# The mean subtraction of three LayerNorm walks moved from GpSimd to VectorE

## The reference

```python
def layernorm(x, g, b):
    mu = jnp.mean(xf, axis=-1, keepdims=True)
    var = jnp.mean(jnp.square(xf - mu), axis=-1, keepdims=True)
    y = (xf - mu) * lax.rsqrt(var + LN_EPS) * g + b

def hybrid_layer(x, ...):
    proj = x @ w_in
    (q_lat, kv_lat, k_rope, g_mla, p_in, g_pool, c_h, c_b, c_c, g_conv) = jnp.split(proj, ...)
    y_mla = mla_mixer(...) * silu(g_mla); y_pool = ...; y_conv = ...
    out = concatenate([y_mla, y_pool, y_conv]) @ w_out + b_out
    return layernorm(DEEPNORM_ALPHA * x + out, ln_g, ln_b)

def first_block(...):
    h = layernorm(x, emb_ln_g, emb_ln_b)
    for l in range(DEPTH):          # DEPTH = 2
        h = hybrid_layer(h, ...)
```

## Time and profile before

| | |
|---|---|
| median of 3 runs | 2504.43 us (2503.02 to 2504.67) |
| profiled execution, its own time | 2505.22 us |
| its span in the trace | 2503.5 us |
| mean granted TensorE clock | 0.986 of full |
| TensorE matmul busy | 2414.2 us (96%) |
| VectorE busy | 1259.9 us (50%) |
| ScalarE busy | 890.3 us (36%) |
| GpSimd busy | 396.5 us (16%) |

### The profile page before, as it was taken

The page is one execution under the profiler, slowest core; times in us unless marked ns, Lnnn a source line. Parts: engine busy times, 40 slices in busy tenths (PEclk is TensorE's granted clock), DMA queues, the critical chain, the costliest instruction groups (busy, mean ns, idle before and its releaser), DMA issues.

```text
span 2503.5 us, 31553 instructions
## 1 busy us (share of the span) xinstructions
PE 2414.2 (96%) x11534; PEld 1977.2 (79%) x11534; DVE 1259.9 (50%) x1794; ACT 890.3 (36%) x1344; POOL 396.5 (16%) x391
## 2 busy tenths in 40 slices
PE   4999999999999999999999999899999999999997
PEld 2888888788888788888788886688878888887886
DVE  8665543366446565444366546635245444444333
ACT  4522222365223522222365223322234444444221
POOL 6400000033003300000042003003002122222000
PEclk8999999999999999999999999999999999999999
DMA  4455554212221455553212222322222222223332
GB/s 141 149 182 169 183 177 133 77 60 67 93 92 67 156 185 170 175 184 126 83 52 68 92 92 101 126 93 93 100 93 68 76 79 80 75 75 100 127 101 75
DMA packets 78280, 277.69 MB, mean 111 GB/s; under 512 B 8832, under 2 KB 9088, under 8 KB 77824
## 3 DMA queue, kind: packets, MB, share of 16 engines
q1 hardware_dynamic: 61344, 213.29, 25.8%
q0 software_dynamic: 16864, 63.45, 7.6%
HBM read 268.31 MB, written 8.39 MB: 111 GB/s over the span
## 4 chain that ended last, share of the span: by engine, by line
PE 80%; issue 9%; DVE 5%; POOL 3%; ACT 2%; DMA 0%; DVEq 0%; ACTq 0%; SPq 0%; POOLq 0%
PE bank L322 25%; PE bank L324 25%; PE bank L323 25%; POOL sum L407 1%; DVE w_lo L317 1%; PE bank L1898 1%; DVE x_lo L1037 1%; POOL probs L394 1%; PE bank L1828 1%; ACT w_hi L294 0%; PE bank L1962 0%; PE bank L1679 0%; PE bank L1680 0%; DVE x_res L1598 0%; PE bank L1963 0%
## 5 line engine op out<-in xcount | busy, mean ns | idle before, releaser
L324 PE MATMUL bank<-x_hi,w_hi 128*128 128x512 f32 x2880 | 1125.6, 391 | 0.0
L323 PE MATMUL bank<-x_hi,w_lo 128*128 128x512 f32 x2880 | 1124.1, 390 | 0.0
L322 PE MATMUL bank<-x_lo,w_hi 128*128 128x512 f32 x2368 | 946.7, 400 | 30.7 <-DVE x_lo L1037 17.2
L317 DVE TENSOR_TENSOR w_lo<-w_raw,w_hi 128x1024 fp32r<-128x1024 f32 (+1 forms) x384 | 483.6, 1262 | 792.7 <-ACT w_hi L294 791.1
L294 ACT ACTIVATE w_hi<-w_raw 128x1024 fp32r<-128x1024 f32 x390 | 407.5, 1048 | 950.6 <-PE bank L324 926.9
L324 PEld LDWEIGHTS bank<-x_hi,w_hi 128*128 128x128 f32 x2880 | 542.0, 188 | 115.3
L323 PEld LDWEIGHTS bank<-x_hi,w_lo 128*128 128x128 f32 x2880 | 543.4, 189 | 107.8 <-issue 2.4
L322 PEld LDWEIGHTS bank<-x_lo,w_hi 128*128 128x128 f32 x2368 | 447.7, 189 | 124.6 <-issue 30.9
L322 PE MATMUL bank<-mix_lo,w_hi 128*128 128x512 f32 x640 | 252.8, 395 | 1.3 <-issue 1.0
L394 POOL TENSOR_SCALAR probs<-probs,stats 128x128 f32<-128x128 f32 (+3 forms) x128 | 138.6, 1089 | 672.7 <-DVE stats L1329 672.6
L322 PEld LDWEIGHTS bank<-mix_lo,w_hi 128*128 128x128 f32 x640 | 120.7, 189 | 27.2 <-issue 1.7
(11 more groups left out here) (304 smaller groups left out, 2268.9 us busy)
## 6 DMA issues: line engine op xcount, KB each, us to landing
w_raw<-stream SPq DMA_DIRECT2D x390, 512.0 KB, 3.5
ada_w<-wada POOLq DMA_DIRECT2D x96, 512.0 KB, 4.6
x_res<-xT SPq DMA_DIRECT2D x16, 256.0 KB, 5.5
x_res_spill<-x_res POOLq DMA_DIRECT2D x8, 512.0 KB, 7.5
x_res<-x_res_spill POOLq DMA_DIRECT2D x8, 512.0 KB, 7.5
outT<-x_res SPq DMA_DIRECT2D x16, 256.0 KB, 2.3
cond_b<-cond POOLq DMA_DIRECT2D x2, 1024.0 KB, 5.2
row_params<-rows POOLq DMA_DIRECT2D x1, 1536.0 KB, 7.5
```

What stands on the lines that cost most here:

```text
L317: nc.vector.tensor_tensor(out=WL[:, slot, :cols[n]], in0=RAW[:, slot, :cols[n]], in1=WH[:, slot, :cols[n]].bitcast(F32), op=ALU.subtract). ...
L322: nc.tensor.matmul(out, wh, xl, start=first, stop=False)
L323: nc.tensor.matmul(out, wl, xh, start=False, stop=False)
L324: return nc.tensor.matmul(out, wh, xh, start=False, stop=last)
```

## The change

VectorE does the subtraction itself, just ahead of its multiplication, in all three walks. `normalise_sub` is gone from GpSimd. What GpSimd waited for, the finished mean and the free buffer, VectorE waits for now.

```diff
@@ GpSimd
-            def normalise_sub(n):
-                pool.wait_ge(S["sh_tot"], n + 1)
-                def sub(k, i=None):
-                    if i is not None:
-                        pool.wait_ge(S["n_x"], norm_uses(n, k) + i * (8 if n < DEPTH else 4))
-                        k = 4 * (i + 1) + k
-                    nc.gpsimd.tensor_tensor(out=NBUF[b][:, :], in0=feature(Y, k), in1=SB[:, :], op=ALU.subtract)\
-                        .then_inc(S["n_sub"], 1)
...
-            normalise_sub(0)
...
-                normalise_sub(l + 1)
@@ VectorE, normalise(n, between)
                     buf = NBUF[k % 4]
+                    if k == 0:
+                        dve.wait_ge(S["sh_tot"], n + 1)
+                    if k >= 4:
+                        dve.wait_ge(S["n_x"], norm_uses(n, k - 4))
+                    TT(out=buf[:, :], in0=Y[:, k, :], in1=SB[:, :], op=ALU.subtract).then_inc(S["n_sub"], 1)
                     dve.wait_ge(S["n_sub"], KT * n + k + 1)
                     TT(out=buf[:, :], in0=buf[:, :], in1=PS[7][:, :], op=ALU.mult).then_inc(S["n_mul"], 1)
```

## The result

The changed kernel takes 2514.61 us in the median of six runs (2509.77 to 2516.29), the kernel before 2504.18 in six runs of the same comparison: +10.4 us, ratio 1.004, 95% interval 1.0029 to 1.0052. The forecast was +4.8, and the stated range ended at 2511.8. The profiled execution took 2514.63 us; its span is 2513.0 us, 9.5 more than before.

What follows compares the result with a forecast made beforehand. TensorE, four fifths of the chain that ended last, was taken to bound the kernel. First walk, clock, second and third walk summed to 0 + 1.2 + 2.4 + 1.2 = 4.8 us: forecast 2509.2 us, range 2504.8 to 2511.8.

Steps and rivals of the forecast that it cites:

- The pace: Time per tile with x_lo in a walk: 1.93 us with VectorE subtracting, against 1.70 before and TensorE's 2.09.
- The first walk: First norm's walk over the tiles: an earlier start but no net change, 0 us, bounds -1.2 and 0.2.
- The gain of about 1.1 is given back whole: First norm: TensorE starts earlier but resumes at 97.1 as before, after waiting 2.4 us instead of 1.31.
- the hold: A VectorE weight split arriving under GpSimd's 16 tensor_scalar looks held until GpSimd is nearly through, 4.85 and 4.74 us.
- The rival in which the split is let in a fixed time after its arrival: Weight split under GpSimd's tensor_scalar: TensorE keeps its own shifts, +1.2 us in all, 2505.6 us; chance 0.13.
- The second walk: Second norm's walk over the tiles: last x_lo and GpSimd's work behind it late, +2.4 us, lower bound +1.16.
- The two waits for the splits: Second norm, around 820: TensorE stalls of 2.0 and 0.7 us for two weight splits.
- The third walk: Third norm, where VectorE squares odd tiles: 3.25 us a pair against 2.91, +1.2 us, bounds 0.9 and 1.6.
- The clock: TensorE's granted clock: one new half-speed stretch after the 2.4 us wait at 97, +1.2 us, bounds 0 and 1.7.
- The forecast for 845: Second norm: TensorE resumes in `lat_sums` at 845.2 instead of 842.84, after a wait of 2.4 us.
- The "clearly slower" rival: Extra half-speed stretch around 820 and full cost at 97: 7.0 us in all, 2511.4 us; chance 0.37.
- The faster rival: All walks: VectorE's step is 1.70 us or less, so the early gains stay: -2.5 us, 2501.9 us; chance 0.05.

Runs made afterwards that it cites:

- e5: The changed kernel with GpSimd's 16 tensor_scalar spread out, one behind each of the first 16 pairs of ada loads: 2502.39 us, ratio 0.9990 to the kernel before.
- e6: The kernel before with GpSimd's 16 tensor_scalar spread out, one behind each of the first 16 pairs of ada loads: 2497.60 us, ratio 0.9977.
- e4: The changed kernel with ten identity products on TensorE ahead of its wait in `lat_sums`: 2508.27 us, ratio 1.0020 to the kernel before.
- e7: The changed kernel with identity products on TensorE in the third walk's gaps and thirty behind its last square: 2508.74 us, ratio 1.0023 to the kernel before.
- e11: The changed kernel with identity products on TensorE both in `lat_sums` and in the third walk: 2505.63 us, ratio 1.0010 to the kernel before.
- e2: The kernel before with VectorE subtracting in the second walk only, GpSimd in the other two: 2507.37 us, ratio 1.0013.
- e8: The kernel before with identity products on TensorE in the third walk's gaps and thirty behind its last square: 2502.54 us, ratio 0.9999.
- e3: The kernel before with VectorE subtracting in the third walk only, GpSimd in the other two: 2507.68 us, ratio 1.0017.

## Why the prediction was wrong

**The pace, right.** Forecast 1.93 us a tile, measured 1.92; first matmul forecast at 53.2, measured at 53.24.

**The first walk, right.** The step "The gain of about 1.1 is given back whole": resume forecast at 97.1 after 2.4 us of wait, measured 97.12 after 2.51. e5 and e6 show the hold by removing it. The rival in which the split is let in a fixed time after its arrival fell: it was held 6.06 and 5.97 us, not 4.85. The Trainium skill says in GPSIMD Engine Reference, Key points, that GpSimd shares its SBUF interfaces with VectorE and contends with instructions that have two SBUF inputs; the trace agrees, 1.23 against 6.06 us for the same split.

**The second walk, right in size.** Forecast +2.4, measured +2.4 (4.1 - 1.7). The two waits for the splits were forecast as 2.0 and 0.7; the second was 0.73, and the first came in pieces of 0.27 and 0.96 us for x_lo and 0.17 for the split, 1.4 in all, since TensorE had already caught up with VectorE's x_lo, which I had not counted on.

**The third walk, a term mis-sized.** Forecast +1.2 with bounds 0.9 and 1.6, measured +1.9. VectorE's own lateness was 1.2 as forecast (last square 1575.19 against 1568.61, less the 5.4 of the row above); missed was that TensorE sums in order, so that it is square 13 which decides and not square 15.

**The clock, the step that failed.** "I count one new half-speed stretch there ... +1.2, bounds 0 and 1.7." One stretch behind 97 did come, at 1.7. But I charged the clock at one place, and the changed kernel loses more than the kernel before at four that cost time: behind 97 (1.7 against 0), behind 847 (3.4 against 1.7), around the first matmul of the second block (5.1 against 3.4) and behind the last wait in its first tiles (1.7 against 0). Only at the first two had the wait ahead of the stretch grown. Together they cost 5.1 us in the trace where 1.2 was forecast; e4, e7 and e11 take this, and what the kernel before loses there too, away by products alone. The forecast for 845 had the longer wait of 2.4 us in it, and charged nothing for it. The "clearly slower" rival came nearer, with 7.0 us, but put its second stretch at 820, where the clock stayed at 1.00. Windows of the changed kernel:

```profile
820.00:830.00 10.00, 7.88 (x31) 5.48 (x31) 9.86 (x15) 7.39 (x11) 0.00 (x0) 1.00 0.35 107
```

The 1.7 for a stretch fitted the one behind 97; the number of places was wrong, and with it the range, which allowed two such stretches.

**The faster rival fell.** VectorE's dependent pair lies 0.71 or 0.72 apart, as the statistics had shown. GPSIMD Engine Reference (the Trainium skill, 4.1 Engine selection) advises VectorE for such an operation. The trace agrees for the instruction, 0.69 us against 1.26 or more on GpSimd in the kernel before, and the kernel is slower all the same.

Open: why a given wait sets off a stretch in one trace and not in another (2.33 us in e2), why the third walk's edit costs clock behind waits that it leaves as they were, and whether the surplus gain of e5 and e6 comes from the places near 500, 788 and 1250 in most executions.

## What to carry to other kernels

Moving work from a slow idle engine to a fast one pays only if the fast one has room per step where the consumer is: here the step went from 1.70 to 1.93 us against a consumer's 2.09, and the slack it used up was what paid for the weight splits. When TensorE is ahead or behind by a microsecond, look at what it waits for next before counting the gain; if that is held by another engine (here a row of GpSimd tensor_scalar), the microsecond comes back as a wait, and a wait may cost its own length again in clock. A change that lengthens several waits should be charged for the clock at each of them, at least in the range, and the cure is to take the wait's cause away (e6, -5.4 us) or to keep TensorE busy over it (e4), as long as the products don't delay what follows (e8 gained nothing).

## What the runs showed of the hardware

The clock's answer to a wait is not a function of its length alone. In e2, behind a wait of 2.33 us that ended at 843.89, it stayed at 1.00; in e3, behind 1.14 us that ended at 842.28, it fell. Windows of e2, and then of e3:

```profile
844.00:848.00 4.00, 4.00 (x22) 3.49 (x23) 3.23 (x8) 0.69 (x2) 0.00 (x0) 1.00 0.75 252
```

```profile
844.00:848.00 4.00, 4.00 (x12) 3.14 (x11) 1.61 (x7) 0.69 (x2) 0.00 (x0) 0.57 0.79 258
```

The same kernel's times fall into groups: those of e2 lie at 2502.5 to 2503.8 (five) and 2507.4 to 2508.8 (six), those of e5 at 2497.9 to 2498.5 (four) and 2501.0 to 2503.0 (seven). The upper group of e2 has mean granted clocks of 0.984 and 0.985, the lower 0.986 to 0.988. The distance of the groups is the size of two or three half-speed stretches, and by it a change of 0.1 or 0.2% of such a kernel can be one of which stretches occur.

Under GpSimd's row of one-input tensor_scalar a weight split of VectorE, which reads two inputs, took up to 6.06 us instead of 1.21, 4.85 more, and ended 0.55 or 0.56 us before the row did in all four cases. Beside GpSimd's two-input subtraction the same split took 2.3 us ahead of tile 4 (2.32 at 801.98), x_lo mostly 1.15 to 1.19 and a square of the third walk up to 1.79, where each of the last two needs 0.68 alone. So the instruction with fewer inputs, in a dense row, held the neighbour longer. The multiplication, with one input in PSUM, took 0.67 to 0.69 in either case.
